# Modulation vectors in the shadow of the first block: row sums moved from TensorE to VectorE

## What is computed

```
sc_x = silu(c); sc_c = silu(c_ctx)
for l in range(DEPTH):                      # 2
    mx = (sc_x @ ada_w[l] + ada_b[l]).reshape(bsz, 6, 1, d)
    mc = (sc_c @ ada_w[l] + ada_b[l]).reshape(6, d)
    hx = modulate(rmsnorm_2(x, norm_g[l, 0]), mx[:, 0], mx[:, 1])
```

## Time and profile before

| | before |
|---|---|
| median of 3 runs | 4350.52 us (4350.52 to 4362.95) |
| the profiled execution | 4354.2 us |
| its span | 4352.4 us |
| TensorE busy (share of the span) | 3966.3 us (91%) |
| VectorE busy | 1848.9 us (42%) |
| ScalarE busy | 1383.7 us (32%) |
| GpSimd busy | 1421.2 us (33%) |
| DMA engines, mean share | 24.6% |
| mean granted TensorE clock | 0.947 |

### The profile page before, as it was taken

The page is one execution under the profiler, slowest core; times in us unless marked ns, Lnnn a source line. Parts: engine busy times, 40 slices in busy tenths (PEclk is TensorE's granted clock), DMA queues, the critical chain, the costliest instruction groups (busy, mean ns, idle before and its releaser), DMA issues. The chain is left out here.

```text
span 4352.4 us, 48704 instructions
## 1 busy us (share of the span) xinstructions
PE 3966.3 (91%) x19562; PEld 3251.2 (75%) x19562; DVE 1848.9 (42%) x3076; ACT 1383.7 (32%) x2082; POOL 1421.2 (33%) x644
## 2 busy tenths in 40 slices
PE   6999998999989999899988888889999879999998
PEld 4777766777667776777766776789999668876886
DVE  4444435553554344474454565231111545543113
ACT  3223334332332333432223443231111334443222
POOL 1224543655422454355541110113222100013442
PEclk9999999999999999999998997899999888999999
DMA  2123332444312233244430000112222100012332
GB/s 85 53 62 96 114 91 68 123 130 129 101 54 65 85 114 92 68 131 126 128 107 27 25 25 15 39 40 63 63 63 59 49 14 15 14 44 72 94 93 77
DMA packets 544397, 316.69 MB, mean 73 GB/s; under 512 B 35828, under 2 KB 517167, under 8 KB 544175
## 3 DMA queue, kind: packets, MB, share of 16 engines
q1 hardware_dynamic: 543903, 312.53, 24.6%
q10 hardware_dynamic: 272, 1.05, 0.1%
HBM read 311.44 MB, written 2.10 MB: 72 GB/s over the span
## 5 line engine op out<-in xcount | busy, mean ns | idle before, releaser
L443 POOL TENSOR_TENSOR wlo<-wraw,whi 128x1024 fp32r<-128x1024 f32 (+5 forms) x640 | 1421.0, 2227 | 2895.8 <-ACT whi L436 2895.1
L459 PE MATMUL acc<-hh,whi 128*128 128x512 f32 (+2 forms) x2744 | 1068.0, 389 | 72.2 <-POOL wlo L443 32.9
L461 PE MATMUL acc<-hh,wlo 128*128 128x512 f32 (+2 forms) x2744 | 1042.5, 380 | 0.0
L460 PE MATMUL acc<-hl,whi 128*128 128x512 f32 (+2 forms) x2744 | 1038.9, 379 | 0.0
L436 ACT ACTIVATE whi<-wraw 128x1024 fp32r<-128x1024 f32 (+5 forms) x640 | 625.1, 979 | 878.4 <-DMA wraw<-in_ada_w 270.0
L459 PEld LDWEIGHTS acc<-hh,whi 128*128 128x128 f32 x2744 | 523.1, 191 | 216.6 <-POOL wlo L443 54.9
L460 PEld LDWEIGHTS acc<-hl,whi 128*128 128x128 f32 x2744 | 523.6, 191 | 91.1 <-issue 10.0
L461 PEld LDWEIGHTS acc<-hh,wlo 128*128 128x128 f32 x2744 | 522.5, 190 | 84.1
L1358 DVE TENSOR_TENSOR t<-acc,sq 128x768 f32<-128x768 f32 (+1 forms) x44 | 36.3, 825 | 501.2 <-PE acc L461 501.2
L459 PE MATMUL ob<-hh,whi 128*128 128x512 f32 (+2 forms) x576 | 218.1, 379 | 11.6 <-DVEq L764 11.3
L660 DVE TENSOR_SCALAR y<-acc 128x512 f32<-128x512 f32 (+1 forms) x80 | 59.6, 745 | 360.6 <-PE acc L461 360.6
(11 more groups left out here) (367 smaller groups left out, 6091.7 us busy)
## 6 DMA issues: line engine op xcount, KB each, us to landing
wraw<-in_ffn_w SPq DMA_DIRECT2D x120, 512.0 KB, 3.8
wraw<-in_w_in SPq DMA_DIRECT2D x102, 512.0 KB, 3.8
wraw<-in_ada_w SPq DMA_DIRECT2D x96, 512.0 KB, 4.0
wraw<-in_w_up SPq DMA_DIRECT2D x88, 512.0 KB, 3.9
wraw<-in_w_down SPq DMA_DIRECT2D x32, 512.0 KB, 4.2
wraw<-in_w_out SPq DMA_DIRECT2D x16, 512.0 KB, 4.0
wraw<-in_w_mkv SPq DMA_DIRECT2D x16, 512.0 KB, 4.1
wraw<-in_ab_w_in SPq DMA_DIRECT2D x14, 512.0 KB, 3.8
```

The lines of the kernel that those rows point to most:

```text
L443: e.tensor_tensor(wlo[0:rows, s, a:b, 0:w], wraw[0:rows, s, a:b, 0:w], whi[0:rows, s, a:b, 0:w].bitcast(F32), ALU.subtract).then_inc(lo_re ...
L459: e.matmul(o, wh, xh, start=first, stop=False)
L460: e.matmul(o, wh, xl, start=False, stop=False)
L461: return e.matmul(o, wl, xh, start=False, stop=last)
```

## The change

The pieces no longer go through ScalarE, GpSimd and the big matmuls. VectorE itself multiplies each piece, as it landed in `wraw`, by the two conditioning columns and adds into two sums of 128 x 512 (one in `row_g` or `row_f`, now 128 partitions high, the other in unused columns of `sq`): four instructions a piece. TensorE adds the sums over the partitions, with eight matmuls a group where there were four. The ring's books are split: a slot that held a piece is free when VectorE has used it (`ada_used`), a slot that held a slab when TensorE has. In the feed-forward units the piece moves: SP loads it in front of the unit's two slabs, and VectorE works on it in front of the unit's first scaling, where its call stood behind the unit. TensorE's calls stay where they were. Core of the diff:

```diff
+        def slot_free(e):
+            n = len(ring)
+            if n >= RING:
+                kind, at = ring[n - RING]
+                e.wait_ge(ada_used if kind == "ada" else slab_done, at)
...
+        def load_ada(e, src):
+            slot_free(e)
+            s, landing = lands(len(ring), 1)
+            adas.append((s, landing))
+            ring.append(("ada", len(adas)))
             e.dma_start(wraw[:, s, :, :].rearrange("p (k a) m -> p k (a m)", k=2), src).then_inc(landed[s], 16)
...
+        def ada_sums(n):
+            at = row_g if n % ADA < 4 else row_f
+            return [at[:, :].rearrange("p (b a) -> p b a", b=2), sq[:, :, SEQ:TC]]

         def pe_ada(e, c):
             n = c.count("ada")
             if n % 4 == 0 and n // 4 % ADA not in ADA_FLUSH:
                 pe_ada_out(e, c)
-            w = weights(e, c)
-            for j in range(2):
-                k = n % 4 * 2 + j
-                for rows in (whi, wlo):
-                    mm = e.matmul(ob[1][0:4, :], sc4[:, k, :], rows[:, w, 4 * j:4 * j + 4, :].rearrange("p a m -> p (a m)"),
-                                  start=k == 0 and rows is whi, stop=k == KT - 1 and rows is wlo)
-            mm.then_inc(slab_done, 1)
...
+        def pe_ada_out(e, c):
+            n = c.count("ada_out")
+            e.wait_ge(ada_row, c.next(ada_row))
+            if n:
+                e.wait_ge(ada_kept, c.next(ada_kept))
+            for j in range(4):
+                for v, sums in enumerate(ada_sums(n)):
+                    mm = e.matmul(ob[0][:, 2 * j + v:2 * j + v + 1], sums[:, j // 2, j % 2 * P:j % 2 * P + P], edge[:, 4, 0:1],
+                                  start=True, stop=True)
+            mm.then_inc(ada_out, 1)

+        def dve_ada(e, c):
+            n = c.count("ada")
+            if n % 4 == 2 and n // 4 % ADA not in ADA_FLUSH:
+                dve_ada_out(e, c)
+            s, landing = adas[n]
+            e.wait_ge(landed[s], landing)
+            if n % 4 == 0 and n:
+                e.wait_ge(ada_out, n // 4)
+            for j in range(2):
+                k = n % 4 * 2 + j
+                w = wraw[:, s, 4 * j:4 * j + 4, :].rearrange("p (b a) m -> p b (a m)", b=2)
+                if k:
+                    e.wait_ge(ada_sum, c.next(ada_sum, 2))
+                for v, sums in enumerate(ada_sums(n // 4)):
+                    col = scT[:, k, v:v + 1]
+                    if k == 0:
+                        ins = e.tensor_scalar(sums, w, col, None, ALU.mult)
+                    else:
+                        ins = e.scalar_tensor_tensor(out=sums, in0=w, scalar=col, in1=sums, op0=ALU.mult, op1=ALU.add)
+                    ins.then_inc(ada_sum, 1)
+            e.wait_ge(ada_sum, c.at(ada_sum, 2))
+            e.sem_inc(ada_used, 1)
             if n % 4 == 3:
+                c.next(ada_sum, 2)
+                e.sem_inc(ada_row, 1)
...
# dve_ffn, one unit
                         if conv:
+                            dve_ada(e, c)
+
                             def wcol(k):
...
                         e.wait_ge(act_ready, c.next(act_ready))
-                        if conv:
-                            dve_ada(e, c)
...
# sp_ffn, one unit
+                        if ada:
+                            sp_ada(e, c)
                         load(e, c, [(0, P, rows_of(up, l, 0, KT, u))])
                         load(e, c, [(0, P, rows_of(up, l, 0, KT, u + FF))])
-                        if ada:
-                            sp_ada(e, c)
```

More of the change, by code:

```diff
@@ L390, in p3, with lands @@
             return ps[0:M, 0:b, 0:n]
-        slabs = []
-        slabs = []
+        slabs, adas, ring, uses = [], [], [], [0] * RING
+        def slot_free(e):
[3 more added lines that the diff above has]
+                e.wait_ge(ada_used if kind == "ada" else slab_done, at)
+        def lands(n, dmas):
+            uses[n % RING] += 16 * dmas
+            return n % RING, uses[n % RING]
         def load(e, c, parts, width=P, cols=None):
-            n = len(slabs)
-            s = n % RING
             tiles = []
@@ L408, in load @@
                 tiles.append((rows, k0, k1))
-            slabs.append((tiles, width * (2 if cols else 1), len(parts)))
-            if n >= RING:
-                e.wait_ge(slab_done, 2 + n - RING + 1)
+            slot_free(e)
+            s, landing = lands(len(ring), len(parts))
+            slabs.append((tiles, width * (2 if cols else 1), s, landing))
+            ring.append(("slab", 2 + len(slabs)))
             for (k0, rows, src), m in zip(parts, cols or [0] * len(parts)):
                 e.dma_start(wraw[0:rows, s, k0:k0 + src.shape[1], m:m + width], src).then_inc(landed[s], 16)
[L415 to L421, removed]
+        def load_ada(e, src):
+            slot_free(e)
+            s, landing = lands(len(ring), 1)
+            adas.append((s, landing))
+            ring.append(("ada", len(adas)))
             e.dma_start(wraw[:, s, :, :].rearrange("p (k a) m -> p k (a m)", k=2), src).then_inc(landed[s], 16)
@@ L432, in head @@
             if n < len(slabs):
-                s, (tiles, w, dmas) = n % RING, slabs[n]
-                e.wait_ge(landed[s], c.next(landed[s], 16 * dmas))
+                tiles, w, s, landing = slabs[n]
+                e.wait_ge(landed[s], landing)
                 for rows, a, b in tiles:
@@ L438, in tail @@
         def tail(e, c, n):
-            s, (tiles, w, _) = n % RING, slabs[n]
+            tiles, w, s, _ = slabs[n]
             for rows, a, b in tiles:
@@ L449, in weights @@
             e.wait_ge(lo_ready, c.next(lo_ready, len(slabs[n][0])))
-            return n % RING
+            return slabs[n][2]
         def passed(c):
@@ L632, in pe_linear_y, with act_linear_y @@
             turns(e, c, KT // 2, body)
-        def act_linear_y(e, c, ada=(), flush=False, T=None, y=None):
+        def act_linear_y(e, c, T=None, y=None):
             if y is not None:
@@ L645, in act_linear_y @@
                      .then_inc(ysq_ready, 1)
[L646 to L649, removed]
         def dve_linear_y(e, c, T, y, first=True, last=True, ada=(), flush=False):
@@ L1231, in pe_ada @@
-            mm.then_inc(slab_done, 1)
[L1232 to L1254, removed]
-            if n % 4 == 3:
[L1256 to L1271, removed]
+                w = wraw[:, s, 4 * j:4 * j + 4, :].rearrange("p (b a) m -> p b (a m)", b=2)
[8 more added lines that the diff above has]
+                    ins.then_inc(ada_sum, 1)
@@ L1322, in act_ffn @@
                     c.next(act_ready, FT if conv else 2)
-                act_linear_y(e, c, ada_down(p) if conv else (), conv and p == 2, T, y if p == len(FF_PARTS) - 1 else None)
+                act_linear_y(e, c, T, y if p == len(FF_PARTS) - 1 else None)
         def dve_ffn(e, c, T, y, ah, al, conv, l=None):
@@ L2241, in constants @@
         edge[:, g, :] = 1.0 / np.minimum(np.arange(PAD) + 1, w)
-    edge[0:4, 4, 1:3] = np.tile(np.eye(2, dtype=np.float32), (2, 1))
     out["edge"] = edge
```

20 lines of the change are left out of this document (7 added, 13 removed).

## The result

The changed kernel takes 4569.67 us (median of four runs, 4567.1 to 4571.81), the kernel before 4351.59 beside it: a ratio of 1.0492, 95% interval 1.0477 to 1.0508, or +218 us. The forecast was 4580, +228.

What follows compares the result with a forecast made beforehand. TensorE was taken to bind the feed-forward and gates before the change. Terms 193 - 8 + 21 + 22 = +228 us on the profiled 4354.2, less 4, gave 4578, rounded to 4580; range 4410 to 4690.

Steps and rivals of the forecast that it cites:

- A regular unit, 15.0: Feed-forward unit that does not begin a group: 15.0 us against 12.13 before, bounds 12.7 and 15.5.
- w: Time from a free ring slot to usable weights: 8.0 us taken after the change, 7.2 for a load alone.
- a second tie closes this to a loop of one unit: Feed-forward: ScalarE rounds both slabs of unit j+1 before unit j's Silu; 12.1 us without GpSimd, 15.2 with it.
- The wait for `ada_out`, 24.6: Feed-forward units beginning a group: VectorE waits for TensorE's previous turning; 24.6 us each, five a layer, bounds 22.7 and 25.5.
- Feed-forward: Feed-forward units of both layers: +193 us (bounds +106 and +217); column loops, a separate term: -8 (bounds -12, 0).
- Turning a group, 2.1: TensorE adding a group's sums over partitions: eight matmuls instead of four, 2.1 us against 1.05, bounds 1.05 and 3.
- Gates, the mis-sized term: Gates loop: next tile's gate 2 waits for VectorE's second piece; 29.6 us against 27.8, +21 altogether (bounds -22, +58).
- The clock: TensorE's lower clock after 10 + 14 longer idles: 0.9 us lost each, +22 us in all (bounds 0, +67).
- The weights stay hidden: Rival, faster: slots come free early enough and TensorE binds throughout, 4276 us; chance 6%.
- Only the `ada_out` waits bind: Rival: regular feed-forward units run at 11.2 us, only group-beginning units stall, 4395 us; chance 14% with mixed cases.
- It cancels: Rival: loops at 12 us and short stalls leave less than 0.3% either way; chance 3%.
- more than forecast: Rival: the lower clock stays after each idle, or turning is dear, over 4690 us; chance 7%.

Runs made afterwards that it cites:

- the piece behind the unit: The changed kernel with the piece back behind its feed-forward unit, in SP's loads and VectorE's program: 4469.94 us, ratio 1.0249 to the kernel before.
- The shifted kernel before: The kernel before with sc4 and row_f moved, so that tiles behind sc4's old place start 128 bytes lower: 4336.61 us, ratio 0.9955.
- the padded changed kernel: The changed kernel with an unused tile of 128 bytes a partition where sc4 stood, restoring later tiles' addresses: 4597.04 us, ratio 1.0537 to the kernel before.
- the two buffers: The changed kernel with a second pair of sum buffers for every other feed-forward group: 4481.35 us, ratio 1.0283 to the kernel before.
- control: The changed kernel run again on another chip without an edit: 4585.84 us, ratio 1.0529 to the kernel before.

## Why the prediction was right, and where it was not

- **Sign and size.** +218 against +228; the mechanism (slots that VectorE frees late) is shown by taking it away: -174 us without the ring, some -100 without the single buffer. That the totals lie 10 us apart is in part luck: the gates with their clock took 17 us more than forecast (51 for 34), and some 28 us came off outside both stages, which the forecast did not have.
- **A regular unit, 15.0.** Measured between first scalings, without the units that hold a stall: 14.9 in layer 0, 15.0 in layer 1, from 12.9 to 16.7. w was 7.6 where 8.0 was taken, the Silu ended 7.2 to 7.3 after the piece as forecast, and one lockout of 2.1 us hit instead of 0.7 + 2.4, so the round through the Silu took 14.3. That the mean is still 15 is due to what the forecast did not have.
- **The failed step: "a second tie closes this to a loop of one unit".** The tie exists, but it doesn't set the unit by itself: with it removed nothing was won. The loop over two units, through TensorE's two slabs and GpSimd's lockouts, comes out as long (29.6 for two, worked out and not shown by a run of its own), and the prediction did not price it. For the piece behind the unit it was the other way round: its 13.4 were a loop over two units and left out the round through ScalarE, 14.4 us in the trace, and the units took 14.1.
- **The wait for `ada_out`, 24.6.** From slab to slab TensorE takes 23.2 there (11.2 for two slabs, 1.9 for turning, 2.5 for the sums, whose first pair is a plain product of 0.49 each, 7.6 for w). Ten stalls of 9.8 to 10.3, in the groups that were listed.
- **Feed-forward.** +192 against 193 - 8 for the column loops and 9 for the clock of ten stalls: 194. The column part came out at about -11 (from the last unit's first scaling to the last column).
- **Turning a group, 2.1.** 836.60 to 838.44, 1.84 us for 16 short matmul records where 8 took 1.05; 128 rows cost no more than 4.
- **Gates, the mis-sized term.** +51 against +21 and 13 of the clock. Seven tiles took 31.4 us each where 29.6 and 0.9 were forecast. In one tile, from VectorE's read of the last branch (483.5) to the piece used (492.6) it was 9.1 (forecast 9.2), to usable weights 7.4 (8.2), and then to the next such read 14.3 where 12.2 was taken: TensorE's first ten matmuls behind its wait of 4.06 started 0.43 apart. The first tile won 1.7 (1.9). VectorE's two reads and TensorE's wait (two timelines):

```profile
483.52 0.69 DVE L2096 TENSOR_TENSOR t<-acc,sq 128x512 f32<-128x512 f32 x1 [2.80 <-PE acc L468]
...
514.35 0.69 DVE L2096 TENSOR_TENSOR t<-acc,sq 128x512 f32<-128x512 f32 x1 [2.80 <-PE acc L468]
```
```profile
500.01 0.79 PE L466 MATMUL acc<-hh,whi 128*128 128x512 f32 x1 [4.06 <-POOL wlo L450]
```

- **The clock.** 0.9 us for an idle was read from waits of 2 us; behind the longer ones it was 2.2 (the gates tile above) and 2.1 (the stall at 848.56: 4.42 us for ten starts, 2.33 at the full clock). In the gates and the feed-forward, 512-column matmuls that start about 0.43 us apart sum to 141 us, against 14 before. A matmul there takes 0.2 of its 0.43 more than at the full clock, so TensorE lost some 58 us more than before, part of it in slack; the clock was priced at 22.
- **Not forecast: -24 in the second block**, 2091.8 to 2068.0 us. 12 of it are the 384-column matmuls, by their spacing. The shifted kernel before took 2075.6 there and the padded changed kernel 2081.1, so the addresses are worth 13 to 16 of the 24; the rest stays open. Without this the forecast would have been low by 14 instead of high by 10.
- **Rivals.** "The weights stay hidden" needed a unit's loop under 11.2 us; with a piece of full work in every unit no kernel's units came under 12.7 on the mean. "Only the `ada_out` waits bind" fell with the two buffers: without those waits the loss was still 2.8%. "It cancels" and "more than forecast" fell with the time itself.
- **The VectorE rate.** The sums took 0.75 each when undisturbed, as the row said, not the 0.59 of the estimate from the Trainium skill (VectorE: DVE Perf Modes, the section on the TRN2 errata), which itself says that this formula predicts too little. With lockouts the mean of all 336 was 0.94, that of the half which adds into `sq` 0.88:

```profile
L1265 DVE SCALAR_TENSOR_TENSOR sq<-wraw,scT,sq 128x512 f32<-128x512 f32 x168 | 148.0, 881 | 0.0
```

## What to carry to other kernels

Before work goes to an idle engine, ask which buffers it will then release, and when in that engine's program: the half-idle VectorE cost 5% because the next loads waited for its turn, and the same work placed where it idles, with buffers of its own, won 1.3%, 0.9% of it by the placing. Where a wait falls between two programs that run at different offsets (here the sums in front of the unit, the turning behind it), lay both orders side by side. If taking away one tie of a loop wins nothing, look for a second loop of the same length before the theory is dropped.

## Not expected of the hardware

- Moving the tiles behind `sc4`'s place by 128 bytes a partition changed the pace of 384-column matmuls from 176.7 to 173.3 ns, in both directions and in both kernels (173.3: after, control, before shifted; 176.7: before, pad); 512-column ones stayed at 233.2 to 233.5 ns. Which tile's address matters wasn't tried.
- A VectorE instruction on SBUF operands that met a GpSimd one took some 2 us more, whichever of these it was: L1365 2.50 for 0.43, L1378 2.74 for 0.69, L1276 2.77 for 0.75, L1354 2.35 for 0.69; the longest sum of the changed kernel (L1265) took 3.27 for 0.75. A wait removed in front of such an instruction can be given back as a lockout.
